# A one-core encoder layer on Trainium2: the memory output projection taken in column halves two tiles apart, and the feed-forward's token sums in two ranges

## What is computed

```python
    om = jnp.einsum('bhqm,bmhd->bqhd', p, mem_v.astype(jnp.float32)).reshape(bx, t, MEM_WIDTH)
    x = x + om.astype(x.dtype) @ w_mo
    h = rmsnorm(x, norm_ffn)
    x = x + jnp.square(jax.nn.relu(h @ w_ffn1)) @ w_ffn2
```

## Time and profile before

| | us |
|---|---|
| median of 3 runs | 1762.79 |
| lowest and highest | 1760.92, 1765.31 |
| the profiled execution's own time | 1764.4 |
| its span, from first to last instruction | 1762.4 |
| its mean granted TensorE clock | 0.985 of full speed |

### The profile page before, as it was taken

The page is one execution under the profiler, slowest core; times in us unless marked ns, Lnnn a source line. Parts: engine busy times, 40 slices in busy tenths (PEclk is TensorE's granted clock), DMA queues, the critical chain, the costliest instruction groups (busy, mean ns, idle before and its releaser), DMA issues. The chain is left out here.

```text
span 1762.4 us, 26833 instructions
## 1 busy us (share of the span) xinstructions
PE 1668.7 (95%) x10590; PEld 1485.2 (84%) x10590; DVE 1178.5 (67%) x1742; ACT 805.6 (46%) x1275; POOL 34.1 (2%) x49
## 2 busy tenths in 40 slices
PE   9999999999999988999989989999999689999998
PEld 8777777889999978888977779999999578787876
DVE  6577777667767699547163876666666576767686
ACT  5587777663434365305272633333333233333344
POOL 1000000000000002001000100000000000000001
PEclk9999999999999999999999989999999899999999
DMA  5322121201021142610361223333334933434322
GB/s 189 83 77 77 49 77 49 77 25 50 26 62 50 50 139 91 251 60 25 103 185 37 108 93 131 134 125 129 133 123 156 341 132 120 156 131 156 120 92 112
DMA packets 157694, 190.50 MB, mean 108 GB/s; under 512 B 5505, under 2 KB 117761, under 8 KB 155522
## 3 DMA queue, kind: packets, MB, share of 16 engines
q1 hardware_dynamic: 157570, 188.79, 32.5%
HBM read 134.58 MB, written 54.20 MB: 107 GB/s over the span
## 5 line engine op out<-in xcount | busy, mean ns | idle before, releaser
L620 PE MATMUL PS<-sbuf_h_hi,sbuf_w_hi 128*128 128x384 f32 x600 | 211.4, 352 | 6.0 <-ACT sbuf_g_N L631 2.7
L622 PE MATMUL PS<-sbuf_h_hi,sbuf_w_lo 128*128 128x384 f32 x600 | 201.5, 336 | 0.0
L621 PE MATMUL PS<-sbuf_h_lo,sbuf_w_hi 128*128 128x384 f32 x600 | 201.3, 335 | 0.0
L2654 PE MATMUL PS<-sbuf_ops_w,sbuf_go_u 128*128 128x512 f32 x448 | 177.6, 397 | 8.7 <-DVE sbuf_gg_X L2742 8.7
L2655 PE MATMUL PS<-sbuf_ops_w,sbuf_go_u 128*128 128x512 f32 x448 | 176.0, 393 | 0.0
L2656 PE MATMUL PS<-sbuf_ops_w,sbuf_go_u 128*128 128x512 f32 x448 | 175.7, 392 | 0.0
L2493 PE MATMUL PS<-sbuf_ops_S,sbuf_ops_w 128*128 128x288 f32 x512 | 153.1, 299 | 11.3 <-ACT sbuf_ff_u L2522 4.6
L2497 PE MATMUL PS<-sbuf_ops_S,sbuf_ops_w 128*128 128x288 f32 x512 | 152.8, 298 | 0.0
L2495 PE MATMUL PS<-sbuf_ops_S,sbuf_ops_w 128*128 128x288 f32 x512 | 152.5, 298 | 0.0
L620 PEld LDWEIGHTS PS<-sbuf_h_hi,sbuf_w_hi 128*128 128x128 f32 x600 | 112.8, 188 | 16.2 <-issue 10.0
L2522 ACT ACTIVATE sbuf_ff_u<-PS 128x576 f32<-128x576 f32 x64 | 41.6, 650 | 177.6 <-DMA uD<-sbuf_ff_sums 97.0
(11 more groups left out here) (317 smaller groups left out, 3920.4 us busy)
## 6 DMA issues: line engine op xcount, KB each, us to landing
sbuf_gg_u<-uD SPq DMA_DIRECT2D x28, 1024.0 KB, 5.2
uD<-sbuf_ff_u SPq DMA_DIRECT2D x16, 1152.0 KB, 4.2
sbuf_ff_raw<-w_ffn SPq DMA_DIRECT2D x16, 1024.0 KB, 6.3
sbuf_gg_B<-w_ffn SPq DMA_DIRECT2D x16, 1024.0 KB, 7.8
sbuf_raw<-w_in SPq DMA_DIRECT2D x28, 512.0 KB, 4.9
uD<-sbuf_ff_sums SPq DMA_DIRECT2D x16, 768.0 KB, 6.2
sbuf_X<-x_prompt SPq DMA_DIRECT2D x16, 512.0 KB, 7.2
xD<-sbuf_X SPq DMA_DIRECT2D x9, 512.0 KB, 2.6
```

The source lines that it names most:

```text
L620: pe.matmul(out, hi, h_hi[:, kb, tok], start=kb == 0, stop=False)
L621: pe.matmul(out, hi, h_lo[:, kb, tok], start=False, stop=False)
L622: last = pe.matmul(out, lo, h_hi[:, kb, tok], start=False, stop=kb == KB - 1)
L2654: pe.matmul(out, u_hi, x_hi, start=first, stop=False, skip_group_check=True)
```

## The change

The stage gets its own three programs, `mo_pe`, `mo_act` and `mo_dve`, in place of `out_pe`, `out_act` and `out_dve` with hooks. A list gives the order of the 18 pairs (half, tile):

```diff
+        CUT = 5 * HT // 9
+        MO_SEQ = [(0, 0), (0, 1)] + [x for t in range(NT - 2) for x in ((1, t), (0, t + 2))] + [(1, NT - 2), (1, SMP)]
+        MO_AT = {x: n for n, x in enumerate(MO_SEQ)}
+        MO_Y = {x: n + 1 for n, x in enumerate(x for x in MO_SEQ if x[1] < SMP)}
...
+        def mo_pe(pe):
...
+                    last = pe.matmul(out, h_hi[:, j, tok], w_lo[s][:, cols], start=False, stop=j == 3)
+                    if t == SMP and j % 2:
+                        last.then_inc(slot_free[s], 1)
...
+                if p and 1 <= t < SMP:
+                    if t == 2:
+                        pe.wait_ge(CN["lo"], len(ogroups))
+                    norm_turn(pe, n_ff, t - 1)
+
+        def mo_act(act):
             for t in range(NT):
...
+                norm_square(act, n_ff, t)
+                if 1 <= t < SMP:
+                    ff_high(act, t - 1)
+                if t == SMP - 2:
+                    w_high(act, 0)
+                    w_high(act, 1)
+            act.wait_ge(N["lo"], 2 * (n_ff.base + SMP - 1))
+            sum_high(act, "S1", 0)
+            w_high(act, 2)
+            ff_high(act, SMP - 1)
+            act.wait_ge(a_sum.sem, a_sum.n(1))
+            sum_high(act, "S2", 0)
+            w_high(act, 3)
+
+        def mo_dve(dve):
...
+            added(0, 0)
+            added(0, 1)
+            f_blocks(dve, 0)
+            for t in range(SMP):
+                added(1, t)
+                if t == SMP - 1:
+                    w_low(dve, 0)
+                norm_mean(dve, n_ff, t)
+                if t == SMP - 1:
+                    w_low(dve, 1)
+                norm_scale(dve, n_ff, t)
+                if 1 <= t < SMP - 1:
+                    ff_low(dve, t - 1)
+                if t + 2 < NT:
+                    added(0, t + 2)
+            added(1, SMP)
+            ff_low(dve, SMP - 2)
+            norm_mean(dve, n_ff, SMP)
+            dve.wait_ge(N["lo"], 2 * (n_ff.base + SMP - 1))
+            sum_raw(dve, "S2", "S1", "A11", 0)
+            norm_scale(dve, n_ff, SMP)
+            sum_low(dve, "S1", 0)
+            w_low(dve, 2)
+            ff_low(dve, SMP - 1)
```

```diff
+            left_over(FF_AT["P1", 0])
+            ff_high(act, SMP)
+            w_high(act, 4)
+            act.wait_ge(N["lo"], 2 * (n_ff.base + NT) - 1)
+            sum_high(act, "S1", 1)
+            w_high(act, 5)
+            left_over(FF_AT["P1", 1])
+            act.wait_ge(a_sum.sem, a_sum.n(2))
+            sum_high(act, "S2", 1)
+            w_high(act, 6)
+            sum_high(act, "S3")
+            w_high(act, 7)
+            w_high(act, 8)
+            left_over(FF_AT["P6", 0])
+            act.wait_ge(a_sum.sem, a_sum.n(3))
+            sum_high(act, "S4")
+            left_over(FF_AT["P7", 0])
+            for k in range(9, 13):
+                w_high(act, k)
...
             for t in range(NT):
-                sp.wait_ge(mo_s[1], NT + t + 1)
+                sp.wait_ge(mo_s[1], MO_AT[1, t] + 1)
                 sp.dma_start(xD[t], X[:, t, :]).then_inc(xl[t], 16)
```

More of the change, by code:

```diff
@@ L1767, in out_pe, with out_act @@
                         norm_turn(pe, norm, t - 2)
-        def out_act(act, round0, nkb, norm, first=lambda act, p: None,
-                    between=lambda t: None, after=None):
+        def out_act(act, round0, nkb, norm, first=lambda act, p: None, between=lambda t: None):
             passes = nkb // 2
@@ L1783, in out_dve @@
         def out_dve(dve, sems, round0, nkb, norm, banks=(4, 5, 6, 7), scaled=lambda dve, p, t: None,
[L1784 removed]
+                    after=lambda dve, p, t: None):
             y, add = sems
@@ L2435, in mo_behind, with part, sum_high, sum_low @@
[L2435 to L2439, removed]
+        def part(x, i):
+            return x[:, :, (0, CUT)[i]:(CUT, HT)[i]]
+        def sum_high(act, x, i=None):
+            hi, raw_ = (a_hi[x], a_raw[x]) if i is None else (part(a_hi[x], i), part(a_raw[x], i))
+            act.activation(hi, raw_, ACT.Copy).then_inc(a_cut.sem, 1)
+        def sum_low(dve, x, i=None):
+            dve.wait_ge(a_cut.sem, a_cut.n(SUM_CUT[x, i]))
+            lo, raw_, hi = (y if i is None else part(y, i) for y in (a_lo[x], a_raw[x], a_hi[x].bitcast(F32)))
+            dve.tensor_tensor(lo, raw_, hi, ALU.subtract).then_inc(a_low.sem, 1)
@@ new lines, in sum_raw @@
+        def sum_raw(dve, x, y, z, i=None):
+            out, p, m = (a_raw[w] if i is None else part(a_raw[w], i) for w in (x, y, z))
+            dve.tensor_tensor(out, p, m, ALU.subtract).then_inc(a_sum.sem, 1)
+        def mo_pe(pe):
+            y, add = mo_s
+            for n, (p, t) in enumerate(MO_SEQ):
+                if t == 0:
+                    for s in pass_slots(p):
+                        wait_unit(pe, unit(R_MO, s), s)
+                if n >= len(MO):
+                    pe.wait_ge(add, n - len(MO) + 1)
+                mo_ready(pe, p, t)
+                out = PS[:, MO[n % len(MO)], :]
+                tok = slice(t * P, (t + 1) * P)
+                for j in range(4):
+                    s = pass_slots(p)[j // 2]
+                    cols = slice((j % 2) * 512, (j % 2 + 1) * 512)
+                    pe.matmul(out, h_hi[:, j, tok], w_hi[s][:, cols], start=j == 0, stop=False)
+                    pe.matmul(out, h_lo[:, j, tok], w_hi[s][:, cols], start=False, stop=False)
+                    last = pe.matmul(out, h_hi[:, j, tok], w_lo[s][:, cols], start=False, stop=j == 3)
+                    if t == SMP and j % 2:
+                        last.then_inc(slot_free[s], 1)
+                if t < SMP:
+                    last.then_inc(y, 1)
+                if p and 1 <= t < SMP:
+                    if t == 2:
+                        pe.wait_ge(CN["lo"], len(ogroups))
+                    norm_turn(pe, n_ff, t - 1)
@@ new lines, in mo_dve, with added @@
+        def mo_dve(dve):
+            y, add = mo_s
+            def added(p, t):
+                n = MO_AT[p, t]
+                if t < SMP:
+                    dve.wait_ge(y, MO_Y[p, t])
+                else:
+                    s = pass_slots(p)[1]
+                    projected(dve, unit(R_MO, s), s)
+                x = X[:, t, p * 512:(p + 1) * 512]
+                dve.tensor_tensor(x, PS[:, MO[n % len(MO)], :], x, ALU.add).then_inc(add, 1)
+            added(0, 0)
[22 more added lines that the diff above has]
+            ff_low(dve, SMP - 1)
@@ L2506, in ff1_act, with left_over @@
         def ff1_act(act):
[L2507 to L2512, removed]
+            def left_over(s):
+                what, n = FF[s]
                 if what in ("P1", "P6", "P7", "P4"):
```

95 lines of the change are left out of this document (40 added, 55 removed).

## The result

| | before | after |
|---|---|---|
| median us (4 runs each) | 1762.84 | 1774.53 |
| lowest and highest | 1760.92, 1765.31 | 1772.50, 1776.45 |
| profiled execution, its span | 1764.4, 1762.4 | 1774.76, 1772.8 |
| mean granted clock | 0.985 | 0.982 |

The changed kernel is slower. Its ratio to the kernel before is 1.0052, 95% interval 1.0037 to 1.0067 (about 9 us; the two medians lie 11.7 apart). The forecast was 1770.9, with slower the likeliest.

What follows compares the result with a forecast made beforehand. PE bounds the kernel, busy 95%, but VectorE (DVE) bounds the feed-forward's start. Late stores delay a weight cut by 8.4 us; 0.3 of slack leaves 8.1, so 1762.8 + 8.1 = 1770.9 us, range 1766.5 to 1777.

Steps and rivals of the forecast that it cites:

- ScalarE's 19 us: ScalarE idle some 19 us before its 256-wide write of S1 over X, ended by a DMA.
- PE's 16 us hole: PE idle about 16 us before the turn of tile 6, waiting for that tile's scaling, then at clock 0.50.
- the holes that went from the feed-forward's start: At the feed-forward's start, PE's 4.59 us hole before product P7 of block 0 was to go.
- signs of being wrong: ScalarE's write before 992, five stores under 8 or over 14 us, or VectorE idle over some 5 us, 1001 to 1059.
- from VectorE's resumption to the add of right 8: VectorE's queue after the stall, from 1001.2 to the add of tile 8's right half at 1014.0: 12.8 us.
- The price of the stores: Five 512 KB stores of X behind the load, each 1.33 us at 397 GB/s; the fifth lands at 1000.5.
- Rival 1: The stores hold no one, so VectorE's weight cut comes 10.0 to 10.4 us earlier: 1752.5 us, faster; chance 0.08.
- the term of 45.2: VectorE from the add of right 8 to the weight cut for P3 of block 1: 43.1 us plus 2.1 of waits.
- the chain I had named: VectorE's weight cut releases SP's load for P1 of block 3; its cut and an output add precede P3 of block 1.
- Rival 1's turning point: The fifth store landing before 992.4, 8.1 us earlier than the forecast 1000.5, would make the change a gain.
- Rival 2: Stall mostly covered: stores pass the load (3.4 us less), VectorE's waits 2 shorter; about 1765.5 us, chance 0.09.
- Rival 3: The stall pulls PE's clock down: products P5 to P3 at 1.2 GHz, +3 to +6 us, about 1775.5; chance 0.2.

Runs made afterwards that it cites:

- e1: Changed kernel with SP's stores of X for tiles 0 to 6 placed ahead of the raw1 load; 1756.19 us against 1763.93 for the kernel before, ratio 0.9954.
- e6: Changed kernel, SP's program untouched, left halves run ahead so slot 1 is freed earlier; 1763.08 us against 1763.52 for the kernel before, ratio 1.0000.
- e5: Kernel before with one added SP wait holding the raw1 load and all stores of X until right 6's add; 1777.02 us against 1763.52, ratio 1.0080.
- e2: Changed kernel with only the stores of X for tiles 0 to 2 ahead of the raw1 load; 1772.62 us, ratio 1.0043 to the kernel before.
- e7: e1 with the four weight sums of block 1 made by GpSimd instead of VectorE; 1754.46 us, ratio 0.9949 to the kernel before.

## Why the prediction was right, and where it was off

**Right, by its own steps.** SP's order is the cause: shown twice from the side of the change (e1 moves the stores, e6 frees the slot earlier, and each takes the loss away) and once from the side of before (e5). The time of the load (990.24 for 988 to 989; counted from the stage's start it is 0.4 us late), the stores on its heels, ScalarE's 19 us, PE's 16 us hole, the holes that went from the feed-forward's start, and P3 of block 1 as the place where the loss comes out are all in the trace. One of the signs of being wrong was touched: more than some 5 us of idle on VectorE between 1001 and 1059. The window has 7.2:

```profile
1001.00:1059.00 58.00, 44.69 (x307) 42.74 (x308) 50.79 (x67) 29.25 (x45) 3.32 (x3) 0.89 0.17 61
```

Of these, 2.3 us lie before VectorE resumed at 1003.31, so they are the stall itself; 4.9 are left behind it, so from there on VectorE was as full as forecast.

**The sizes.** Counted from the stage's start, P3 of block 1 is 10.0 us later than before (133.13 against 123.11), where 8.1 was forecast. The terms: the load left at 49.95 us instead of 49.5 (+0.4); from its issue to ScalarE's write 12.4 and not 11.9 (+0.5); from VectorE's resumption to the add of right 8 13.0 for 12.8 (+0.2); from there to the weight cut of P3 of block 1 (1062.21) 45.9 for 45.2 (+0.7). In this last term VectorE was busy 44.0 us and idle 1.9, for 43.1 and 2.1 in the sum. The terms make 1.8 of the 1.9 us.

**The price of the stores.** I took 397 GB/s from a window of one us. The windows of after (columns as in the earlier trace rows) have the queue at 420 from 996 on, but only at 277 from 992 to 996, while the load was in it:

```profile
992.00:996.00 4.00, 0.88 (x4) 0.38 (x3) 0.00 (x0) 0.00 (x0) 0.00 (x0) 1.00 0.95 277
996.00:1000.00 4.00, 0.00 (x0) 0.00 (x0) 0.00 (x0) 0.00 (x0) 0.00 (x0) 0.66 1.03 420
```

From the load's issue to ScalarE's write after has 12.4 us with five stores and e2 8.8 with two. By that difference a store cost 1.2 us (I had 1.33) and the rest 6.4 (I had 5.2), and the load landed after 6.0 us, for 5.4 before. So the stores were cheaper than I took them and the load dearer, and the two partly cancelled. The Trainium skill ("DMA: Bandwidth & Descriptors", Specifications) gives 358 GB/s as HBM limit per core; further down, under Measured, the same page calls it a core's share when both cores of a pair stream, and has 425 for one core and 16 MB. This kernel runs on one core, and the trace agrees with the second figure: 420 from 996 to 1000.

**Rivals.** Rival 1 named the gain without the stall, 1752.5, 10.3 us below before. Its mechanism is e1, which gained 8.1 by its ratio (O: 8.9). At O 1.4 us are missing. Half of them come before the add of right 8, which stood at 57.1 us from the start (995.5 on my scale is 56.4), the other half behind it, where the term of 45.2 was again 45.9. The end of the stage is the chain I had named. ScalarE in e1:

```profile
1046.40 0.65 ACT L2594 ACTIVATE sbuf_ff_u<-PS 128x576 f32<-128x576 f32 x1 [9.77 <-DMA uD<-sbuf_ff_sums]
...
1049.26 0.63 ACT L2317 ACTIVATE sbuf_ops_w<-sbuf_ff_raw 128x512 fp32r<-128x512 f32 x1 [1.14 <-DMA sbuf_ff_raw<-w_ffn]
```

The wait of 9.77 us for the stores of u of block 0 is the long one, but the one that ends last is 1.14 for the load, which left at 1043.22 behind VectorE's weight cut; before had the same two, 6.89 and 1.46 us. Rival 1's turning point, a landing before 992.4, was nearly right: by the slope from e1 to after (19.2 us of O for 19.5 of W) I estimate that O equals that of before at W = 51.9 us, 991.0 on the scale of before. Rival 2 did not come: no store passed the load. Rival 3 did not come either: the clock fell, as the forecast itself had it, but was back before P5 to P3, where the rival wanted it low, and cost nothing. When the hole ended at 1009.68 the clock was at 0.50, and it rose within the next window (the columns again those of the earlier trace rows):

```profile
1005.00:1010.00 5.00, 0.32 (x2) 0.32 (x3) 3.07 (x6) 3.15 (x6) 0.55 (x1) 0.50 0.26 105
1010.00:1015.00 5.00, 5.00 (x18) 4.29 (x17) 4.02 (x8) 2.12 (x4) 0.93 (x1) 0.57 0.26 105
```

Only the turn of tile 6 and the first half of right 8 fell into it: right 8's matmuls follow each other at 0.43 us till 1014.0 and at 0.23 from 1014.4 on, and P1, which the prediction had at the lower level too, ran at the upper one. VectorE was later than PE anyway, as the prediction had it: PE waited 2.18 us for it before P1 of block 1. P5 to P3 ran at 2.4 GHz.

**Where the expected gain went.** The change does what it is made for (8 us, e1) and pays 17 to 19 for a transfer that it never mentions.

## What to carry to other kernels

An engine's list of transfers is a queue of waits. When an order of work is changed, go through every wait of that list and ask when its event now comes and what stands behind it, even where the diff does not touch it. Here one load that nobody needed for 10 us more (in e1 it left at 989.50, and its first block was cut at 1000.32) stood, with a new late wait, ahead of five stores that were needed at once; placing the load after those stores turned +0.5% into -0.5%. And two changes that look like one are worth timing apart: the order of the start gave 5.4 of the 8.9 us at O, the split in ranges none that could be measured.

## What the runs showed of the hardware

- **GpSimd and VectorE hold each other up.** In e7 GpSimd's second sum, begun right behind its first, took 1.75 us from start to start. Its first took 4.11 and its third 3.67: both began while VectorE worked on an instruction with two inputs in SBUF, and both ended 1.1 to 1.2 us after the last such instruction of VectorE (1022.56, the end of the weight cut of 1021.88, and 1027.88, the end of the cut of S4). The other way, VectorE's cut of S4 began at 1024.26, inside GpSimd's second (till 1025.43), and took 1.06 us more than its 2.56 elsewhere; the squares of 1023.26 and 1028.58 and the weight cut of 1029.82 (till 1031.34; GpSimd's fourth ended at 1030.79) were stretched likewise. VectorE's add from PSUM at 1027.80, with one input in SBUF, was not slowed, 0.74. It looks as if the later one waits for the earlier one's end. By the Trainium skill, "SBUF — State Buffer", section Who interferes with whom, the two share a port pair as an exclusive lock, the second to issue blocks, and a VectorE instruction with at most one input in SBUF, outside its two-port modes, is spared; the trace agrees, with 1.06 us lost where 1.17 were left of GpSimd's instruction, and nothing at the add from PSUM.
- **The path to the stage varies.** The same instructions took 937.45 to 943.08 us up to the stage's first matmul in the profiled executions shown. A single profile of this kernel can't show a gain of 3 us by its absolute times; counted from the start of the stage, repeated parts agree to 0.1 us (W at 42.8 or 42.9 in five kernels).
